# Products of ones in TensorE's order at its waits, in a two-block transformer kernel

## Chip, cores and metric

The kernel runs on one core of one Trainium2 chip. The metric is device time in microseconds of one execution, the median of several. Lower is better. PE stands for TensorE's matmuls, PEld for its weight loads, DVE for VectorE, ACT for ScalarE, POOL for GpSimd.

## Reference

`first_block` runs two layers over x of 512 tokens by 1024, with a context of 256 tokens; `second_block` runs two more layers over the result. Cut to what matters:

```python
# first_block, each layer: RMS norm, mixer, RMS norm, MLP
hx = rms_norm(x, norm1_g) * (1 + mod_x[1]) + mod_x[0]          # hc likewise, 256 context tokens
# layer 0: hybrid_mixer (mLSTM heads and a gated short conv); layer 1: attention_mixer
#   grouped attention: 16 query heads, 4 key and value heads of 64,
#   q and k normed per head and rotated, 512 queries against 256 + 512 keys, softmax, output
x = x + mod_x[2] * y_x
x = x + mod_x[5] * sqrelu_mlp(rms_norm(x, norm2_g) * (1 + mod_x[4]) + mod_x[3], w1, w2)
# second_block, each layer: h = x @ w_in; three branches (latent attention, differential
#   attention, memory attention), each gated and summed; then
x = layernorm(ALPHA * x + merged @ w_out)
x = layernorm(ALPHA * x + square(relu(x @ w1)) @ w2)
```

## The kernel before

All is float32. Activations lie transposed in SBUF, features on the 128 partitions in 8 chunks k, tokens in the columns. A product of float32 accuracy is three products of rounded halves (`mm3`, L1183 to L1185): Hh or Gh with Wh, the same with the low part Wl, and the low part Hl or Gl with Wh. Weights stream in blocks of 1024 columns through two slots; ScalarE rounds each to Wh (L384), GpSimd subtracts to make Wl (L262). `project_block` multiplies a block with a set of token segments.

Each engine has its order of work written out by hand in one program; semaphores tie them. PE takes PSUM banks 0 to 3 in turn: `tiles.take(pe)` waits until VectorE has freed the bank. Banks 4 to 7 have fixed uses. `wait_ready` waits for VectorE's `for_pe`.

The places that the change touches are these.

`rms_stats` sums squares over the features with products of one output column (L1278, L1283), waits for the roots from VectorE and broadcasts them over partitions into banks 4 and 5 (`spread_tokens`, L1240). It runs before the hybrid layer (there with `last_apart` false), before its MLP, before attention, and before the second MLP. `layer_stats` does the same for a layer norm of the second stage, with four column sums (L1230), then `spread(6, shift)` and `spread(4, root)`, each behind a `wait_ready`; it runs twice a layer.

`project_first` follows a norm. It takes its banks, then for each k waits for the normed chunk H from VectorE and ScalarE and multiplies one or two weight blocks with it. It runs eight times: in the hybrid layer, in the four MLPs, at the start of attention, and at the start of the two layers of the second stage.

`attention_pe` works through 4 groups g of 8 turns u. A turn is `scores(g, u)` into banks 4 to 7 (L1593), on odd turns then `output` (weights by values), then `turned_weights(u - 1)`, twelve transposes (L1606). `scores` waits for the exponentials of the turn before (ACT L766), since it writes over the banks that they read. In groups 0 to 2 projections of the next group's keys and queries stand between the turns; in group 3 nothing does. `square_sums(0)` (L1635, L1638) sums squares of keys and queries: it takes a bank, then waits for `raw_done`. It runs once ahead of the groups and at turn 3 of groups 0 to 2.

`onesr` holds ones, 128 by 128, in the rounded type; the hybrid layer uses it for sums.

Of the kernel before, what the change touches and what calls it, by code (L numbers as in the profile page):

```python
# [23 lines left out]
P = 128  # L24
# [306 lines left out]
def latent_scratch(v):  # L331

    M = v["M"]
    kv, kv_sq, q_sq = ([M[:, t * SEQ:(t + 1) * SEQ] for t in ts] for ts in ((0, 1), (2, 3), (4, 5, 6)))
    return kv, kv_sq, q_sq, M[:, 7 * SEQ:8 * SEQ], v["sc"][:, 48:52], v["sc"][:, 52:56]


def layer_norm_scratch(v):

    M, sc = v["M"], v["sc"]  # L340
    scaled = [M[:, i * SEQ:(i + 1) * SEQ] for i in range(KT)]
    return scaled, [sc[:, at:at + 4] for at in (32, 36, 40, 56)], sc[:, 0:8]


def last_squares(v):

    return v["M"][:, 3328:4096]
# [5 lines left out]
    return [M[:, at + TOK * i:at + TOK * (i + 1)] for i in range(3)]  # L353


SINE_TILES = (2, 3, 4, 5)
OUT_ORDER = (4, 5, 0, 1, 2, 3, 6, 7)
CENTRED = ((), (), (), (), (0, 1, 2), (3, 4), (5, 6), (7,))
# [7 lines left out]
def act_program(nc, block, v, n_blocks, extra):  # L366
# [5 lines left out]
    def _(act):  # L372
# [60 lines left out]
        def updated_squares(k, segs):  # L433
            act.wait_ge(for_act, wants.next())
            squares(k, segs)
# [207 lines left out]
        for m in range(KT):  # L643
            used_squared(m, X_SEGS)
            if m < KT - 1:
                updated_squares(m, X_SEGS)
            if m in SINE_TILES:
                t = SINE_TILES.index(m) ^ 1
                act.wait_ge(for_act, wants.next())
# [496 lines left out]
def pe_program(nc, block, v, n_blocks):  # L1146
    Hh, Hl, Gh, Gl, Wh, Wl = (v[n] for n in ("Hh", "Hl", "Gh", "Gl", "Wh", "Wl"))
    Ph, Pl, Qh, Ql, Kh, Kl, Vh, Vl = (v[n] for n in ("Ph", "Pl", "Qh", "Ql", "Kh", "Kl", "Vh", "Vl"))
    psum, S0, S1, M, tab, diag, onesr = (v[n] for n in ("psum", "S0", "S1", "M", "tab", "diag", "onesr"))
# [3 lines left out]
    def _(pe):  # L1153
        tiles = Tiles(v["tile_done"], v["loops_entered"], v["bank_free"])
# [10 lines left out]
        def arriving(width=P):  # L1165

            s = n_block[0] % 2
            n_block[0] += 1
            before = low.next(QUARTERS) - QUARTERS
            return tuple(w[:, s].rearrange("p (k m) -> p k m", m=width) for w in (Wh, Wl)), before  # L1170

        def wait_quarter(before, k):
            pe.wait_ge(v["w_low"], before + k // 2 + 1)
# [4 lines left out]
        def wait_ready(n=1):  # L1178
            pe.wait_ge(v["for_pe"], ready.next(n))

        def mm3(dst, a, b, first, last):

            pe.matmul(dst, a[0], b[0], start=first, stop=False)  # L1183
            pe.matmul(dst, a[0], b[1], start=False, stop=False)  # L1184
            return pe.matmul(dst, a[1], b[0], start=False, stop=last)  # L1185
# [19 lines left out]
        def project_first(*segs_of):  # L1205

            ws = [arriving() for _ in segs_of]
            banks = [[tiles.take(pe) for _ in segs] for segs in segs_of]
            for k in range(KT):
                wait_ready()  # L1210
                for (w, before), segs, bs in zip(ws, segs_of, banks):
                    if k % 2 == 0:
                        wait_quarter(before, k)
                    for b, (t0, n) in zip(bs, segs):
                        mm = mm3(psum[:, b, 0:n], (w[0][:, k, :], w[1][:, k, :]),
                                 (Hh[:, k, t0:t0 + n], Hl[:, k, t0:t0 + n]), k == 0, k == KT - 1)
                        if k == KT - 1:
                            mm.then_inc(v["tile_done"], 1)
# [4 lines left out]
            pe.matmul(psum[0:dst_rows, b, 0:n], lhsT, rhs, start=True, stop=True).then_inc(v["tile_done"], 1)  # L1223

        H, G = (Hh, Hl), (Gh, Gl)

        def column_sums(b, at, x):

            for qt in range(4):
                mm = pe.matmul(psum[:, b, at + qt:at + qt + 1], x[:, qt * P:(qt + 1) * P], ones[:, 0:1], start=True, stop=True)  # L1230
            return mm

        def squares_made():
            pe.wait_ge(v["squared"], squared.next())

        def spread_tokens(bank, col):

            n = col.shape[1]
            for i in range(n):
                mm = pe.matmul(psum[:, bank, i * P:(i + 1) * P], col[:, i:i + 1].broadcast_to([P, P]), ident, start=True, stop=True)  # L1240
            mm.then_inc(v["spread_done"], 1)

        def spread(bank, col):

            wait_ready()
            spread_tokens(bank, col)
# [9 lines left out]
        def layer_stats():  # L1256

            b = tiles.take(pe)
            wait_ready()
            column_sums(b, 0, S0)  # L1260
            wait_ready()
            column_sums(b, 4, S1)
            wait_ready()
            column_sums(b, 8, v["X"][:, KT - 1, X0:TOK])
            squares_made()
            column_sums(b, 12, last_squares(v)).then_inc(v["tile_done"], 1)
            _, (_, shift, _, root), _ = layer_norm_scratch(v)
            spread(6, shift)
            spread(4, root)

        def rms_stats(segs, last_apart=True):

            wait_ready()
            b = tiles.take(pe)
            tt = 0
            for S, (_, n) in zip((S0, S1), segs):
                for i in range(n // P):
                    mm = pe.matmul(psum[:, b, tt:tt + 1], S[:, i * P:(i + 1) * P], ones[:, 0:1], start=True, stop=True)  # L1278
                    tt += 1
            if last_apart:  # L1280
                squares_made()
                for i in range(tt):
                    mm = pe.matmul(psum[:, b, tt + i:tt + i + 1], last_squares(v)[:, i * P:(i + 1) * P], ones[:, 0:1], start=True, stop=True)  # L1283
            mm.then_inc(v["tile_done"], 1)
            wait_ready()
            for lo, hi, c in SPANS[2 - len(segs):]:
                spread_tokens(5 - c, v["sc"][:, 40 + lo // P:40 + hi // P])
# [25 lines left out]
        def mlp(segs, beside=None):  # L1313
            n = len(segs)
            project_first(segs, segs)
            for m in range(2, KT):
                project_block(H, segs)
            with loop(3, 16 * n, 16, KT * n):
                back(segs)
                for m in range(KT):  # L1320
                    project_block(H, segs)
            back(segs, beside)
# [88 lines left out]
        def head_spread(bank, j, done):  # L1411
# [4 lines left out]
            mm.then_inc(done, 1)  # L1416

        rms_stats(ALL_SEGS, False)
        project_first(ALL_SEGS)
        all_head_values()  # L1420
        point, weighed = 0, Count(2 + ML_GIVEN)
        for h in range(ML_HEADS):
# [31 lines left out]
            for group, g0, n in ((0, 0, CTX), (1, X0, SEQ)):  # L1454
# [22 lines left out]
                for step, (kt, dirs) in enumerate(steps + ((None, ""),)):  # L1477
                    if kt is not None:
                        b = tiles.take(pe)
# [39 lines left out]
        for m in range(2, KT):  # L1519
            project_block(G, ALL_SEGS)  # L1520
        rms_stats(ALL_SEGS)
        mlp(ALL_SEGS)

        rms_stats(ALL_SEGS)
        diff_counts = DiffCounts()
        attention_pe(pe, v, tiles, project_block, project_first, mm3, exact, diff_counts)
        wait_ready()
        for m in range(KT):
            project_block(G, X_SEGS)
# [3 lines left out]
        for l in range(2):  # L1533
            _, kv_sq, q_sq, kv_diag, _, _ = latent_scratch(v)
# [31 lines left out]
            for m in range(KT):  # L1566
                project_block(G, X_SEGS, per_k=1 if m == 0 else 0, ks=OUT_ORDER)
                centre(m)
            layer_stats()
            mlp(X_SEGS, centre)  # L1570
            layer_stats()


def attention_pe(pe, v, tiles, project_block, project_first, mm3, exact, counts):
    psum, hand, ident, ones, bones, rot0 = (v[n] for n in ("psum", "hand", "ident", "ones", "bones", "rot0"))
    H, G, Ph, Pl = (v["Hh"], v["Hl"]), (v["Gh"], v["Gl"]), v["Ph"], v["Pl"]
    Qh, Ql, Kh, Kl, Vh, Vl = (v[n] for n in ("Qh", "Ql", "Kh", "Kl", "Vh", "Vl"))
    exp, k32, k2, q_raw, q_sq, v_raw = attention_views(v)[:6]
    keys_scaled = Count()

    def scores(g, u):

        q = slice(u % 4 * P, (u % 4 + 1) * P)
        if g or u:
            pe.wait_ge(v["exps_done"], counts.exps_done.next(2))
        if u % 4 == 0:
            pe.wait_ge(v["operands_ready"], counts.operands_ready.next())
        for c in range(2):
            k = slice(c * HALF, (c + 1) * HALF)
            for i, (x, y) in enumerate(((Qh, Kh), (Qh, Kl), (Ql, Kh))):  # L1590
                for a in range(2):
                    rows = slice(64 * a, 64 * a + 64)
                    mm = pe.matmul(psum[:, 4 + 2 * a + c, 0:HALF], x[rows, q], y[rows, k], start=i == 0, stop=i == 2)  # L1593
                    if i == 2:
                        mm.then_inc(v["scored"], 1)
# [32 lines left out]
    def square_sums(t):  # L1628

        b = tiles.take(pe)  # L1630
        pe.wait_ge(v["raw_done"], counts.raw_done.next(3 if t == 0 else 1))
        at = 0
        if t == 0:
            for tt in range(6):
                pe.matmul(psum[:, b, at:at + 1], k2[:, tt * P:(tt + 1) * P], bones[:, 0:1], start=True, stop=True)  # L1635
                at += 1
        for qt in range(4):
            mm = pe.matmul(psum[:, b, at:at + 2], q_sq[t][:, qt * P:(qt + 1) * P], bones[:, 0:P:64], start=True, stop=True)  # L1638
            at += 2
        mm.then_inc(v["tile_done"], 1)  # L1640
# [1924 lines left out]
```

## Time and profile before

| | |
|---|---|
| median of 3 runs | 4126.87 us (4126.64 to 4128.65) |
| the profiled execution | 4128.24 us, of which 4126.5 us from the first to the last instruction |
| mean granted TensorE clock | 0.973 |
| PE busy | 3920.7 us, 95% of the span |
| PEld, DVE, ACT, POOL busy | 80%, 49%, 36%, 39% |

The granted clock is a share of full speed: 1.00 is 2.4 GHz and 0.50 is 1.2 GHz. A matmul's duration in the rows holds the time in which it overlaps the one before; the distance between starts is its price.

### The profile page before, as it was taken

How to read it: one execution, taken by the hardware profiler on the slowest of the kernel's cores; microseconds unless marked ns; L12 is line 12 of the kernel's file. 1: busy time of each engine (PE TensorE's matmuls, PEld its weight loads, DVE VectorE, ACT ScalarE, POOL GpSimd, SP SyncE). 2: the span in 40 equal slices, each digit the busy share in tenths (PEclk: the TensorE clock that was granted, in tenths of full speed). 3: DMA queues.
4: the chain of work that ended last, by engine and by line, in shares of the span. 5: the costliest groups of instructions: out<-in, count | busy, mean ns of one | idle time of the engine just before them, and what ended most of it. 6: DMA issues, size and time to landing. Idle time of an engine off the chain costs nothing.

```text
span 4126.5 us, 58926 instructions
## 1 busy us (share of the span) xinstructions
PE 3920.7 (95%) x20508; PEld 3307.5 (80%) x20508; DVE 2031.4 (49%) x3318; ACT 1495.4 (36%) x2438; POOL 1628.2 (39%) x2044
## 2 busy tenths in 40 slices
PE   7999899999988889999999999999989999999998
PEld 6888799999977668887677788788867777887887
DVE  5566652332457763335837723532467475225225
ACT  3222231111245542223636633322255465333222
POOL 2111133433321025665242355565632423545665
PEclk9999999999989989999999999999999999999999
DMA  4433211111110012222121122222211211222222
GB/s 174 145 137 138 85 60 67 62 66 61 57 36 21 16 44 92 97 97 93 41 77 57 57 92 94 75 97 97 93 61 43 80 52 60 101 90 77 97 97 97
DMA packets 92744, 328.26 MB, mean 80 GB/s; under 512 B 10240, under 2 KB 12544, under 8 KB 92544
## 3 DMA queue, kind: packets, MB, share of 16 engines
q1 hardware_dynamic: 90928, 323.61, 22.3%
q8 instruction: 135, 2.21, 0.2%
q10 hardware_dynamic: 1616, 1.90, 0.2%
q14 instruction: 65, 0.53, 0.0%
HBM read 323.38 MB, written 2.10 MB: 79 GB/s over the span
## 4 chain that ended last, share of the span: by engine, by line
issue 60%; POOL 30%; PE 8%; DVE 1%; POOLq 1%; ACT 0%; DVEq 0%
POOL Wl L262 30%; PE psum L1183 3%; PE psum L1184 3%; PE psum L1185 3%; POOLq L257 0%; POOLq L259 0%; DVE S L2068 0%; DVE M L2246 0%; DVE X L2068 0%; DVE X L2202 0%; PE psum L1230 0%; PE psum L1240 0%; DVE X L2263 0%; POOLq L262 0%; ACT hand L394 0%
## 5 line engine op out<-in xcount | busy, mean ns | idle before, releaser
L262 POOL TENSOR_TENSOR Wl<-raw,Wh 128x256 fp32r<-128x256 f32 x2040 | 1628.0, 829 | 2491.9 <-ACT Wh L384 2491.4
L384 ACT ACTIVATE Wh<-raw 128x1024 fp32r<-128x1024 f32 x510 | 539.9, 1059 | 1595.9 <-PE psum L1185 1573.8
L1183 PE MATMUL psum<-Hh,Wh 128*128 128x512 f32 (+1 forms) x2704 | 1034.2, 382 | 43.7 <-DVEq L2111 16.8
L1184 PE MATMUL psum<-Hl,Wh 128*128 128x512 f32 (+1 forms) x2704 | 1014.3, 375 | 0.0
L1185 PE MATMUL psum<-Hh,Wl 128*128 128x512 f32 (+1 forms) x2704 | 1014.1, 375 | 0.0
L1183 PE MATMUL psum<-Gh,Wh 128*128 128x512 f32 (+3 forms) x2032 | 747.7, 368 | 12.9 <-DVE Gl L2756 4.6
L1185 PE MATMUL psum<-Gh,Wl 128*128 128x512 f32 (+3 forms) x2032 | 742.9, 366 | 0.0
L1184 PE MATMUL psum<-Gl,Wh 128*128 128x512 f32 (+3 forms) x2032 | 742.7, 365 | 0.0
L1183 PEld LDWEIGHTS psum<-Hh,Wh 128*128 128x128 f32 x2704 | 518.4, 192 | 147.9 <-issue 50.9
L1185 PEld LDWEIGHTS psum<-Hh,Wl 128*128 128x128 f32 x2704 | 516.9, 191 | 71.7
L1184 PEld LDWEIGHTS psum<-Hl,Wh 128*128 128x128 f32 x2704 | 518.9, 192 | 67.9 <-issue 1.3
L1183 PEld LDWEIGHTS psum<-Gh,Wh 128*128 128x128 f32 (+1 forms) x2032 | 381.2, 188 | 71.8 <-DVEq L2111 8.3
L1185 PEld LDWEIGHTS psum<-Gh,Wl 128*128 128x128 f32 (+1 forms) x2032 | 381.1, 188 | 51.4
L1184 PEld LDWEIGHTS psum<-Gl,Wh 128*128 128x128 f32 (+1 forms) x2032 | 381.3, 188 | 50.0 <-issue 0.5
L2068 DVE TENSOR_TENSOR hand<-hand 128x512 f32<-128x512 f32 (+1 forms) x160 | 111.6, 698 | 433.1 <-ACT hand L394 415.7
L2267 DVE SCALAR_TENSOR_TENSOR X<-psum,mod,X 128x256 f32<-128x256 f32 (+1 forms) x160 | 83.9, 548 | 341.4 <-PE psum L1185 340.2
L2263 DVE SCALAR_TENSOR_TENSOR X<-X,psum 128x512 f32<-128x512 f32 x64 | 44.0, 687 | 244.9 <-PE psum L1185 243.8
L2297 DVE TENSOR_TENSOR Gl<-hand,Gh 128x512 fp32r<-128x512 f32 (+1 forms) x160 | 155.4, 971 | 5.5
L2077 DVE CAST Gh<-hand 128x512 fp32r<-128x512 f32 (+1 forms) x160 | 117.7, 736 | 5.5
L2068 DVE TENSOR_TENSOR S<-psum,hand 128x512 f32<-128x512 f32 x32 | 22.1, 692 | 196.2 <-PE psum L1185 195.7
L985 ACT ACTIVATE stage<-psum,soft 128x512 f32<-128x512 f32 x128 | 86.7, 686 | 73.6 <-DVE soft L3144 73.6
L394 ACT ACTIVATE hand<-psum 128x512 f32<-128x512 f32 (+3 forms) x180 | 90.4, 525 | 33.6 <-DVEq L2114 29.6
(353 smaller groups left out, 4489.4 us busy)
## 6 DMA issues: line engine op xcount, KB each, us to landing
raw<-in_wstream SPq DMA_DIRECT2D x510, 512.0 KB, 3.2
stage<-in_ada SPq DMA_DIRECT2D x80, 512.0 KB, 4.1
M<-in_ada SPq DMA_DIRECT2D x16, 512.0 KB, 5.3
X<-in_xT SPq DMA_DIRECT2D x1, 2048.0 KB, 15.1
out<-X SPq DMA_DIRECT2D x8, 256.0 KB, 2.0
X<-in_ctxT SPq DMA_DIRECT2D x1, 1024.0 KB, 10.3
M<-in_memT ACTq DMA_DIRECT2D x1, 1024.0 KB, 5.8
M<-in_axial ACTq DMA_DIRECT2D x1, 512.0 KB, 5.6
```

Of the source, the lines that this page charges most:

```text
L262: pool.tensor_tensor(Wl[:, s, c], raw[:, s, c], Wh[:, s, c].bitcast(F32), ALU.subtract).then_inc(w_low, 1)
L384: act.activation(Wh[:, s], raw[:, s], ACT.Copy).then_inc(v["w_high"], 1)
L394: last = act.activation(hand[p, s, cols], one, func, **k)
L985: last = act.activation(stage[:, s, c * SEQ:(c + 1) * SEQ], psum[:, 4 + 2 * j + c, :], ACT.Exp, bias=soft[:, 4 * j + c:4 * j + c + 1], acc ...
L1183: pe.matmul(dst, a[0], b[0], start=first, stop=False)
L1184: pe.matmul(dst, a[0], b[1], start=False, stop=False)
L1185: return pe.matmul(dst, a[1], b[0], start=False, stop=last)
L2068: do(dve.tensor_tensor(dst, x, y, op))
L2077: do(dve.tensor_copy(dst, x))
L2263: last = dve.scalar_tensor_tensor(out=X[:, m, t0:t0 + n], in0=X[:, m, t0:t0 + n], scalar=1.0, in1=psum[:, b, 0:n], op0=ALU.mult, op1=ALU.add)
L2267: last = dve.scalar_tensor_tensor(out=X[:, m, lo:hi], in0=psum[:, b, lo - t0:hi - t0], scalar=mod[:, part, m, c:c + 1], in1=X[:, m, lo:hi] ...
L2297: do(dve.tensor_tensor(Gl[:, m, t0:t0 + w], r, Gh[:, m, t0:t0 + w].bitcast(F32), ALU.subtract))
```

## The change

A helper issues n products of ones with ones, 512 columns each, into a bank whose content is written anew before anybody reads it. Nobody reads them. Calls stand in PE's order at these places: after the sums of squares in `rms_stats` (4, when `last_apart`), between the two broadcasts of `layer_stats` (3), in `project_first` behind the taking of the banks and ahead of the first wait for H (7), in `square_sums(0)` behind the taking of the bank (5), ahead of the first scores (12), and ahead of the scores of turn 1 of group 0 and of the odd turns of group 3 (6). In the last kind they first wait until the next bank is free. No wait and no other instruction is removed or moved.

```diff
+CLOCK_ROOTS, CLOCK_SHIFTED, CLOCK_NORMED, CLOCK_SCORES, CLOCK_SQUARES = 4, 3, 7, 6, 5
...
             banks = [[tiles.take(pe) for _ in segs] for segs in segs_of]
+            keep_clock(banks[0][0], CLOCK_NORMED)
             for k in range(KT):
                 wait_ready()
...
+        def keep_clock(bank, n):
+
+            for _ in range(n):
+                pe.matmul(psum[:, bank, :], onesr[:], onesr[:].unsqueeze(1).broadcast_to([P, 4, P]), start=True, stop=True)
...
             spread(6, shift)
+            keep_clock(4, CLOCK_SHIFTED)
             spread(4, root)
...
             mm.then_inc(v["tile_done"], 1)
+            if last_apart:
+                keep_clock(5, CLOCK_ROOTS)
             wait_ready()
...
+    def next_bank():
+
+        b = tiles.at % 4
+        pe.wait_ge(tiles.free[b], tiles.uses[b].base + tiles.uses[b].k + 1)
+        return b
+
     def scores(g, u):
 
         q = slice(u % 4 * P, (u % 4 + 1) * P)
+        if g == 3 and u % 2 or (g, u) == (0, 1):
+            keep_clock(next_bank(), CLOCK_SCORES)
         if g or u:
             pe.wait_ge(v["exps_done"], counts.exps_done.next(2))
+        elif u == 0:
+            keep_clock(4, 2 * CLOCK_SCORES)
...
         b = tiles.take(pe)
+        if t == 0:
+            keep_clock(b, CLOCK_SQUARES)
         pe.wait_ge(v["raw_done"], counts.raw_done.next(3 if t == 0 else 1))
```

## Rows read from the trace of the kernel before

**Rows 1.** The page: granted TensorE clock in 40 equal slices, in tenths.

```profile
PEclk9999999999989989999999999999999999999999
```

**Rows 2.** PE in order of time, second stage: start, us, instruction [idle before].

```profile
1901.09 0.39 PE L1185 MATMUL psum<-Gh,Wl 128*128 128x512 f32 x1
1901.32 0.39 PE L1183 MATMUL psum<-Hh,Wh 128*128 128x512 f32 x1
...
1960.79 0.67 PE L1223 MATMUL psum<-S,const 96*96 96x512 f32 x1 [2.06 <-ACT S L894]
...
3072.08 1.37 PE L1223 MATMUL psum<-S,const 96*96 96x512 f32 x2 [2.07 <-ACT S L894]
...
3074.09 0.63 PE L1185 MATMUL psum<-Ph,Wl 128*128 128x512 f32 x1
3074.52 0.63 PE L1183 MATMUL psum<-Ph,Wh 128*128 128x512 f32 x1
```

**Rows 3.** PE's waits over the span: us in total, times, longest us.

```profile
PE psum L1593 <- ACT stage L766: 15.0, 5, 3.5
```

**Rows 4.** Windows in attention: us, PE busy (records), clock, DMA.

```profile
1427.49:1435.98 8.49, 8.49 (x44) 0.80 0.01 2
1442.68:1452.06 9.38, 9.38 (x44) 0.71 0.00 0
1458.09:1466.56 8.47, 8.47 (x44) 0.80 0.01 3
1472.59:1482.36 9.77, 9.77 (x42) 0.68 0.00 0
1226.02:1232.96 6.94, 6.94 (x43) 1.00 0.10 35
...
1176.00:1181.00 5.00, 5.00 (x18) 0.50 0.01 3
1212.60:1226.00 13.40, 13.39 (x72) 0.87 0.00 1
```

**Rows 5.** PE in order of time, in attention.

```profile
1175.65 0.69 PE L1593 MATMUL psum<-Kh,Qh 64*128 64x384 f32 x2 [5.71 <-DVE Ql L2902]
...
1189.13 0.44 PE L1593 MATMUL psum<-Kh,Qh 64*128 64x384 f32 x2
...
1212.61 1.50 PE L1635 MATMUL psum<-const,tab 128*128 128x1 f32 x12 [1.43 <-DVE Gl L2108]
...
1427.49 0.67 PE L1593 MATMUL psum<-Kh,Qh 64*128 64x384 f32 x2 [2.38 <-ACT stage L766]
...
1442.68 0.69 PE L1593 MATMUL psum<-Kh,Qh 64*128 64x384 f32 x2 [3.50 <-ACT stage L766]
```

**Rows 6.** Windows in the latent branch, columns as in rows 4.

```profile
1960.00:1970.00 10.00, 7.83 (x39) 1.00 0.12 45
1963.12:1967.30 4.18, 3.00 (x21) 1.00 0.00 0
```

**Rows 7.** VectorE in order of time, at three places.

```profile
1426.25 1.29 DVE L2108 TENSOR_TENSOR Gl<-psum,Gh 128x512 fp32r<-128x512 f32 x2
...
588.44 2.44 DVE L2171 SCALAR_TENSOR_TENSOR Hl<-M,mod,Hh 128x256 fp32r<-128x256 f32 x4
...
1556.07 1.65 DVE L2171 SCALAR_TENSOR_TENSOR Hl<-M,mod,Hh 128x512 fp32r<-128x512 f32 x2
```

**Rows 8.** Windows from first to last product of project_first, columns as in rows 4.

```profile
575.83:595.11 19.28, 19.28 (x96) 0.86 0.00 1
1547.79:1561.80 14.01, 14.00 (x48) 0.78 0.19 57
...
2634.02:2649.08 15.06, 14.30 (x48) 0.83 0.00 1
...
3746.22:3761.28 15.06, 14.46 (x48) 0.81 0.00 0
```

**Rows 9.** PE in order of time, between two broadcasts of a layer norm.

```profile
3741.47 2.08 PE L1240 MATMUL psum<-const,sc 128*128 128x128 f32 x8 [0.60 <-DVEq L2111]
```

More of the change, by code:

```diff
@@ L1525, in _ @@
         diff_counts = DiffCounts()
-        attention_pe(pe, v, tiles, project_block, project_first, mm3, exact, diff_counts)
+        attention_pe(pe, v, tiles, project_block, project_first, mm3, exact, diff_counts, keep_clock)
         wait_ready()
@@ L1571, in _, with attention_pe @@
             layer_stats()
-def attention_pe(pe, v, tiles, project_block, project_first, mm3, exact, counts):
+def attention_pe(pe, v, tiles, project_block, project_first, mm3, exact, counts, keep_clock):
     psum, hand, ident, ones, bones, rot0 = (v[n] for n in ("psum", "hand", "ident", "ones", "bones", "rot0"))
```

## Prediction

> **What bounds the kernel now.** I read the page first, then the waits of TensorE (PE), then PE's order of time with the granted clock beside it. PE is busy nearly all the time, and the row of its clock shows no digit but 8 and 9 [rows 1]. The mean grant of 0.973 means that some 2 x 0.027 x 4126.5 = 223 us of the span ran at the lower of the two levels, 1.2 GHz, 0.50 in the records, and the rest at 2.4 GHz. At the lower level a product of 512 columns starts 0.43 us after the one before it, at the upper one 0.22 to 0.23 us [rows 2], so I take 0.225 us for a filler at full clock, 0.43 at half clock, and 1 - 0.225/0.43 = 0.48 us for each busy microsecond at half clock as its price. The price is paid only where PE is what the next step waits for. The clock falls behind waits of PE; the longest repeated one in attention is the wait of the scores for the exponentials, 15.0 us in five waits [rows 3]. So the reader is to see three things at each place where fillers stand: is there a wait before which they stand, does the clock stay up with them, and would PE's speed behind the wait have mattered.
>
> **Attention, last group, odd turns (four places, six fillers each).** From the scores to the end of the transposes behind them PE runs without a stop. With the same work and the clock at 1.00 this takes 6.94 us; the four turns in question take 8.49, 9.38, 8.47 and 9.77 us at clocks of 0.68 to 0.80 [rows 4]. Their prices are 1.55, 2.44, 1.53 and 2.83 us, 8.35 in all, and they count in full: what follows (evictions, maxima, exponentials, next odd turn) starts from the last transposes. Six fillers take 6 x 0.225 = 1.35 us, well inside the 3.50 us of the second place [rows 5]; the third and fourth waits have the same form. They leave some 2.0 to 2.15 us idle. Is that short enough? The nearest rows disagree: after a wait of 2.06 us the clock stayed at 1.00, after one of 2.07 us the products came 0.43 us apart [rows 2, 6]. So the fall is not abolished, it is made rarer: of the 6.8 us of these three I take three fifths, 4.1, with bounds of 0 and 6.8. The first place differs. Its fillers first wait for a bank, which VectorE frees with the first of its two L2108 subtractions, at about 1426.25 + 0.65 = 1426.9 [rows 7]; six fillers from there end at 1428.3, and the scores could have gone at 1427.49 [rows 5]. Cost 0.8, gain 1.55 (bounds 0 and 1.55).
>
> A page of the Trainium skill speaks against this part. Transposes, says "TensorE: Matmul & The Clock Gate", Part 4, do not count as PE activity as other products do. By that rule the idle time here would be longer by the 1.5 to 2 us of transposes ahead of the wait, and the clock would fall as before: the gain of 4.1 would be nothing. The trace does not bear it out, since a stretch of 4.18 us of nothing but transposes and a wait had a clock of 1.00 [rows 6].
>
> **Attention, opening scores (12 fillers).** They take 2.7 of the 5.71 us [rows 5] and leave 3.0, too long to hold the clock in most cases, but the low stretch should begin later. 5 us and more behind the wait were at 0.50 [rows 4], worth 2.4; I take half, 1.2 (0 to 2.4).
>
> **Attention, second turn (six fillers).** The scores at 1189.13 follow the projection without a wait [rows 5]. The fillers stand in PE's way: 1.35 us lost, and the exponentials of this turn are what the next scores wait for.
>
> **Attention, square sums (five fillers, four places).** The fillers stand behind the wait for the bank. In three of the four places that is the wait that ends last (1.43 us, ended by VectorE's L2108 freeing the bank [rows 5]); nothing is left to hide them: 3 x 5 x 0.225 = 3.4 us lost. Behind it the clock is 0.87 over 13.4 us [rows 4], that is 3.5 us at half clock, 1.7 us of price, some 5 us for three places. The fillers break an idle stretch with narrow products behind it; I take half, 2.5 (0 to 5). The first of the four stands in a real wait, but narrow products and another long wait follow, and I put it at 0.
>
> **Norms ahead of project_first (seven fillers, eight places; four more in the three RMS norms).** Here what matters is who sets the pace. In the MLP after the first block the last H is ready at 588.44 + 2.44 = 590.88 [rows 7]; a hop of 0.25 and 12 products of 384 columns follow. 96 of them took 19.28 us at 0.86 [rows 8], 5.4 us of it low; 13.9 + 5.4/1.91 = 16.7, or 0.174 each at full clock. So it could end at 593.2 instead of 595.11: 1.9 us. In the next MLP, 1557.72 + 0.25 + 6 x 0.225 = 1559.3 instead of 1561.80: 2.5 us. I take both whole, 4.4 (0 to 4.4), because the four fillers, the spread products and the seven fillers together make PE dense from the sums on, and the clock can be back before the projection. The broadcasts in the three RMS norms may run partly at full clock: 0.9 us (0 to 3). The other places give nothing. In the second stage the projection is paced by VectorE: 15.06 us at a clock of 0.83 and 15.06 at 0.81 [rows 8], each with waits at its end that take up what the slow start lost; the attention's and the first one are of that kind. And the first latent projection of the second stage has no wait at all: L1183 on H follows L1185 on G after 0.23 us [rows 2], so its seven fillers are a loss of 7 x 0.225 = 1.6 us.
>
> **Layer norms (three fillers, four places).** Between the two broadcasts PE waits 0.60 us in the best of the four cases [rows 9], and the eight records of one take 2.08 us. I read that as half clock, since only narrow products ran for some 6 us before. Three fillers at 0.43 are 1.29 us, so each time the second broadcast is 0.7 to 1.3 us late; I take 0.9, 3.6 in all; the last of the four goes straight into the kernel's tail. The denser work may bring the clock back within the second broadcast: I take 1.8 (0 to 3.6).
>
> **Sum.** Gains 4.1 + 1.55 + 1.2 + 2.5 + 4.4 + 0.9 + 1.8 = 16.45. Costs 0.8 + 1.35 + 3.4 + 1.6 + 3.6 = 10.75. Net 5.7 us faster. The profiled execution took 4128.24 us (span 4126.5), 1.4 above the median of 4126.87; taken from the median this is 4121.
>
> **Rivals.** *Everything is kept (4111).* Each row of fillers is enough to hold or to restore the clock: the gains take their upper ends, 1.55 + 6.8 + 2.4 + 5 + 4.4 + 3 + 3.6 = 26.75, less 10.75 is 16.0. For it: one wait of 2.06 us that did no harm. Against it: the one of 2.07 that did. *Gains and costs cancel (4127).* A stretch at half clock need not move with the work: if work starts 1 us sooner and the stretch ends when it would have ended anyway, that 1 us is run at half clock and about half of the gain is gone again. Then some two thirds of the gains remain, 10.75 of 16.45. For it: many low stretches of the same length behind waits of 1.4 to 3.5 us. *Slower (4137).* Products of ones with ones, whose result is the same each time, do not hold the clock; then only the costs are left, 10.75 us, at the places with no wait. It decides from the point at which less than 2.5 us of the gains come true. For it: no row shows such products alone in a wait. Against it: nothing in the rows ties the grant to values rather than to columns that move.
>
> **How the numbers follow.** My forecast, a gain of 2 to 12 us, has 0.52; everything kept 0.22; cancelled 0.13; slower 0.09; something unseen 0.04. A measurement here tells about 0.2% from nothing, 8.25 us, so the line is at 4118.6. Two fifths of the forecast's chance lie beyond it, 0.21; with the first rival that is 0.43 for faster. Slower by that much: the last rival and half of the unseen, 0.11. Within it: 0.46. The range of 4110 to 4129 takes in the forecast, the first two rivals, and the spread that the moments of the falls bring.
>
> **What would show it.** Right: turns of the last group near 7 us from scores to transposes in most but not all of the three later places, and the first with its scores later than now behind the bank; the MLP projections ending 1.3 to 1.6 us after the last H but for the hop; fillers without a wait ahead of them at the first latent projection, at the second turn and behind three bank waits; the second stage's projections still 15.06 us long. Wrong: the clock at 1.00 through all of attention's last group and the layer norms (4111), or 0.50 behind waits filled with fillers just as before (4137).

## Result and profile after

The changed kernel takes 4142.74 us, median of ten runs (4135.52 to 4147.0); the kernel before, beside it, 4128.84 us (4126.64 to 4131.99). The ratio is 1.0031, 95% interval 1.0023 to 1.0039: 12.8 us slower (9.5 to 16.1), by more than the 0.2% set as the line. The forecast was 4121, the range 4110 to 4129.

The page after: span, busy times, granted clock and the queue of instructions; then one group of TensorE's (PE's) waits.

```profile
span 4140.5 us, 59206 instructions
PE 3953.4 (95%) x20650; PEld 3324.3 (80%) x20650; DVE 2026.4 (49%) x3318; ACT 1495.8 (36%) x2438; POOL 1629.1 (39%) x2044
PEclk8999999999999999999999999999999999999999
q8 instruction: 154, 2.52, 0.3%
```

```profile
PE psum L1613 <- ACT stage L767: 7.8, 4, 2.2
```

The wait of the scores for the exponentials fell from 15.0 us [rows 3] to 7.8, and the mean clock went from 0.973 to 0.974. The row to stop at is the fourth: queue q8 carries instructions, and it moved 154 packets instead of 135. (Before, its row on the page is "q8 instruction: 135, 2.21, 0.2%": packets, MB, share.)

To see where the time went I took the start of the same product in both profiled executions and subtracted. These are the differences (after less before), in us, by the place in the kernel before:

| up to | what lies there | change | sum |
|---|---|---|---|
| 560 | hybrid layer | +0.5 | 0.5 |
| 620 | first MLP's norm and projection | -1.0 | -0.5 |
| 1100 | its hardware loop | +8.9 | 8.4 |
| 1186 | attention up to the opening scores | -3.3 | 5.1 |
| 1240 | second turn, first square sums in the groups | +3.0 | 8.1 |
| 1420 | groups 0 to 2 | -2.6 | 5.5 |
| 1545 | group 3, output projection | +1.2 | 6.6 |
| 1600 | second MLP's norm and projection | -1.9 | 4.8 |
| 1902.5 | first latent projection | +1.6 | 6.4 |
| 2615 | rest of the first layer's branches | -0.2 | 6.3 |
| 2656 | layer norm 1 | +2.1 | 8.4 |
| 3020 | layer norm 2 | +2.1 | 10.5 |
| 3730 | second layer's branches | -0.8 | 9.7 |
| 3766 | layer norm 3 | +2.3 | 12.0 |
| 4113 | layer norm 4 | +2.1 | 14.1 |

The largest term is at a place that the prediction does not name. PE in order of time at the end of the loop's first and second trip, after the change (start, us, instruction, idle before it):

```profile
778.62 0.34 PE L1186 MATMUL psum<-Hh,Wl 128*128 128x384 f32 x1
781.80 0.44 PE L1184 MATMUL psum<-Gh,Wh 128*128 128x384 f32 x1 [2.84 <-POOL Wl L262]
...
783.02 0.52 PE L1184 MATMUL psum<-Gh,Wh 128*128 128x384 f32 x1
```

```profile
919.08 0.44 PE L1184 MATMUL psum<-Gh,Wh 128*128 128x384 f32 x1 [2.31 <-POOL Wl L262]
```

L1186 is the last product of the loop's body, L1184 on G its first: TensorE stands still for 2.84 and 2.31 us at the jump back, 137 us apart, and from 783.0 to 786.2 the products then start 0.32 us apart instead of 0.17. GpSimd is named as the releaser, but it had finished that block's Wl at 775.4 (771.81 + 3.57), so it was something that the semaphores do not show.

```profile
771.81 3.57 POOL L262 TENSOR_TENSOR Wl<-raw,Wh 128x256 fp32r<-128x256 f32 x4 [4.67 <-ACT Wh L385]
```

The queue of instructions in this stretch, before and after (packets, MB, share):

```profile
q8 instruction: 1, 0.02, 0.0%
```

```profile
q8 instruction: 19, 0.31, 0.5%
```

These are the rows for 770 to 1060 us. Before, code came for the first trip, and then a single packet at 1045 us, at the end of the third: both jumps back were passed without any. After, all three trips fetched theirs.

### The profile page after: what moved, and what is told of

It reads as the page before. It is cut to its first block, busy times and chain, and to the rows that moved or that the text cites. A ratio compares the mean times of both kernels' runs of the same rounds, so it can differ in the third digit from the quotient of the medians.

```text
span 4140.5 us, 59206 instructions
## 1 busy us (share of the span) xinstructions
PE 3953.4 (95%) x20650; PEld 3324.3 (80%) x20650; DVE 2026.4 (49%) x3318; ACT 1495.8 (36%) x2438; POOL 1629.1 (39%) x2044
## 3 DMA queue, kind: packets, MB, share of 16 engines
q8 instruction: 154, 2.52, 0.3%
## 4 chain that ended last, share of the span: by engine, by line
issue 60%; POOL 30%; PE 8%; DVE 1%; POOLq 1%; ACT 0%; DVEq 0%
POOL Wl L262 30%; PE psum L1184 3%; PE psum L1186 3%; PE psum L1185 3%; POOLq L257 0%; POOLq L259 0%; DVE S L2090 0%; DVE M L2268 0%; PE psum L1247 0%; PE psum L1237 0%; DVE X L2090 0%; DVE X L2224 0%; DVE X L2285 0%; POOLq L262 0%; ACT hand L395 0%
## 5 line engine op out<-in xcount | busy, mean ns | idle before, releaser
L1184 PE MATMUL psum<-Hh,Wh 128*128 128x512 f32 (+1 forms) x2704 | 1027.3, 380 | 33.7 <-DVEq L2133 9.3
L1186 PE MATMUL psum<-Hh,Wl 128*128 128x512 f32 (+1 forms) x2704 | 1006.6, 372 | 0.0
L1184 PE MATMUL psum<-Gh,Wh 128*128 128x512 f32 (+3 forms) x2032 | 750.5, 369 | 17.6 <-POOL Wl L262 9.3
L1186 PE MATMUL psum<-Gh,Wl 128*128 128x512 f32 (+3 forms) x2032 | 745.5, 367 | 0.0
L1184 PEld LDWEIGHTS psum<-Hh,Wh 128*128 128x128 f32 x2704 | 512.3, 189 | 146.9 <-issue 28.0
L1186 PEld LDWEIGHTS psum<-Hh,Wl 128*128 128x128 f32 x2704 | 511.7, 189 | 70.8
L1184 PEld LDWEIGHTS psum<-Gh,Wh 128*128 128x128 f32 (+1 forms) x2032 | 383.0, 188 | 77.2 <-POOL Wl L262 9.1
L1186 PEld LDWEIGHTS psum<-Gh,Wl 128*128 128x128 f32 (+1 forms) x2032 | 382.8, 188 | 51.8
```

## Experiments

A packet of q8 is 2.52 MB / 154 = 16.4 KB. The loop's body in the built program has 768 products of two instructions each and 91 others, 1627 in all. Code that is fetched in blocks can touch one block more or less according to where it begins. 36 instructions, 18 products with their weight loads, stand ahead of this loop in the change. The Trainium skill ("Advanced Engine Details and Errata", ISA Cache) gives blocks of 16 KB with 256 instructions and room for 128 KB of them on TensorE; the size of the packets agrees, and by it the body is six blocks and 91 instructions. This is where the blocks of 256 in the expectations come from. All ratios below are to the kernel before, run beside each.

**1. Nothing but place.** Edit to the kernel before:

```diff
+        for _ in range(36):
+            pe.sem_inc(v["pad"], 1)
         pe.wait_ge(v["consts_loaded"], 32)
```

> The kernel before, with 36 instructions more at TensorE's very start (each adds 1 to a semaphore that nobody waits for; TensorE waits 6.8 us there anyway). That is as many instructions as the 18 products of ones with their weight loads that stand ahead of the first MLP's hardware loop in the changed kernel. No product of ones anywhere. Theory A (place of the code): the loop's body now straddles one more block of 16 KB, is fetched anew in each of its three trips (packets of the instruction queue q8 between 756 and 1045 us, where the kernel before has none), TensorE stands still for 2 to 3 us at both back-edges and half clock follows; 7 to 9 us slower than before, about 4136. Theory B (the products themselves, or weights that come late behind them, make the gaps): nothing changes, within 1 us of before, no q8 packets in the loop.

1.0011 (1.0002 to 1.0020), 4.5 us slower. q8 moved 19 packets between 770 and 1060 us, and PE stood still at both jumps:

```profile
784.53 0.60 PE L1184 MATMUL psum<-Gh,Wh 128*128 128x384 f32 x1 [2.80 <-POOL Wl L263]
...
922.11 0.43 PE L1184 MATMUL psum<-Gh,Wh 128*128 128x384 f32 x1 [2.60 <-POOL Wl L263]
```

The loop is 7.6 us longer than before in this trace, without one product of ones in the kernel. Theory B falls. The median is 4.5 us slower where A said 7 to 9, though the interval reaches to 8.3 us.

**2. All products, moved by a block.** The changed kernel with two such rows of 110 increments.

> The changed kernel with 220 such instructions more, 110 at TensorE's start and 110 in its 7.7 us wait for a transfer at 13 us; with the 36 of the 18 products that makes 256, one block of 16 KB, so that the first MLP's loop lies in its blocks as it did before. Theory A: the two gaps at the back-edges (2.84 and 2.31 us) and the half clock behind them are gone; 7 to 9 us faster than the changed kernel, about 4134, still 5 us slower than before through the layer norms. Theory B: no change, 4142.

1.0065 (1.0051 to 1.0078), 26.9 us slower. The loop is as before (0.0 us of change, no packet in its second and third trip), but the increments cost 18 us: the first product starts at 17.87 us instead of 6.81, and the one behind the wait for a transfer at 37.60 instead of 20.65. So the fetches and the gaps follow the place of the code; the time says little.

**3. No products in the layer norms.** `CLOCK_SHIFTED` 0.

> The changed kernel without the three products between the two broadcasts of the four layer norms. Theory A (these three run at half clock in the way of the second broadcast, 1.3 us each time less the 0.2 to 0.6 us of wait there): 0.7 to 1.3 us in each of four places, 3 to 5 us faster than the changed kernel, about 4138.5. Theory B (the loss of 2.0 to 2.6 us per layer norm is theirs alone): 8 to 10 us faster, about 4133.5. Theory C (it is the earlier fall of the clock that costs, by its phase): less than 1 us.

1.0014 (1.0005 to 1.0023): 5.8 us slower than before instead of 12.8, so 7.0 us for the twelve products, between A and B. The two intervals allow some 2 to 12 us, so the time alone does not tell A from B; the traces say more. First layer norm of the changed kernel:

```profile
2626.82 0.95 PE L1237 MATMUL psum<-const,S 128*128 128x1 f32 x8
...
2630.14 1.87 PE L1237 MATMUL psum<-const,X 128*128 128x1 f32 x8 [0.71 <-DVEq L2133]
...
2634.64 2.08 PE L1247 MATMUL psum<-const,sc 128*128 128x128 f32 x8 [0.93 <-DVEq L2133]
2636.36 1.63 PE L1232 MATMUL psum<-onesr 128*128 128x512 f32 x3
2637.79 1.91 PE L1247 MATMUL psum<-const,sc 128*128 128x128 f32 x8
```

And the same norm in a kernel without the three (the eighth below), where the clock fell at the same sums:

```profile
2614.68 0.94 PE L1238 MATMUL psum<-const,S 128*128 128x1 f32 x8
...
2617.99 1.87 PE L1238 MATMUL psum<-const,X 128*128 128x1 f32 x8 [0.71 <-DVEq L2134]
...
2622.49 3.78 PE L1248 MATMUL psum<-const,sc 128*128 128x128 f32 x16 [0.92 <-DVEq L2134]
```

From the first sum to the end of the broadcasts it is 2639.70 - 2626.82 = 12.88 us with them and 2626.27 - 2614.68 = 11.59 without: 1.29 us, three times 0.43, none of it hidden. A further 1 us comes with the moment at which the clock falls (a share of C): third sums of 1.87 us are at half clock, of 1.05 at full. In the profile of the changed kernel it fell there in all four norms, in that of before in none of them fully. In the other traces, with and without the three products, it was a mixture.

**4. Only attention.** The other counts are 0.

> The changed kernel with only its products in attention (12 ahead of the first scores, 6 ahead of the second turn's and of the four odd turns of the last group, 5 ahead of the square sums); none in the norms. Nothing stands ahead of the first MLP's loop. Theory A (attention gains a little, the loop's place and the norms cost): 1 to 2 us faster than before, about 4127, no q8 packets in the loop. Theory B (attention's gains are eaten by its costs, as in my rival): 0 to 3 us slower than before.

1.0005 (0.9996 to 1.0014), 2 us slower, nearer B, though the interval holds no change as well. In the loop one packet, as before.

**5. No products in layer norms, none ahead of the loop.** `normed` and `roots` are counts per call of `project_first` and `rms_stats`, in the program's order.

```diff
+        normed, roots = [0, 0, 7, 7, 7, 7, 7, 7], [0, 4, 4]
-            keep_clock(banks[0][0], CLOCK_NORMED)
+            keep_clock(banks[0][0], normed.pop(0))
-                keep_clock(5, CLOCK_ROOTS)
+                keep_clock(5, roots.pop(0))
```

> The changed kernel without the three products in the layer norms (as in the third experiment) and without the 18 ahead of the first MLP's loop (7 in the hybrid layer, 4 and 7 at the first MLP). Theory A (the loop's code, +7.6 to +8.9 us in three traces that have it fetched anew): no q8 packets between 757 and 1047 us, no gap at the back-edges; against the third experiment 8.5 us less, plus 1.0 us for the gain at the first MLP's start that is given up: 1.0014 becomes 0.9996, about 2 us faster than before. Theory B (the loop's gaps were of a chance kind, or cost less in the run without a profile): no change against the third experiment, about 6 us slower than before.

1.0009 (1.0000 to 1.0018), 3.7 us slower. A was right about packets (one, as before) and gaps (none) and wrong about the time: 2 us less than the third instead of 7.5, with intervals of 3.7 us either way on both. The trace shows a loop 8.5 us shorter than the third's. That the fetches cost less in the median than in the profiled execution, as Theory B also allowed, is not ruled out.

**6. Only the places that could pay.**

```diff
+        normed, roots = [0, 0, 7, 7, 0, 0, 0, 0], [0, 4, 4]
-        if g == 3 and u % 2 or (g, u) == (0, 1):
+        if g == 3 and u in (3, 5, 7):
-        if t == 0:
-            keep_clock(b, CLOCK_SQUARES)
```

> As the kernel above, and also without the products that stand where TensorE waits for nothing, or behind the wait that ends last: square sums, second turn, the first odd turn of the last group, and all of the second stage. Left are 12 ahead of the first scores, 6 ahead of turns 3, 5 and 7 of the last group, and 4 and 7 at attention's norm and the second MLP's. Theory A (square sums and second turn cost 2.7 to 3.6 us, the first latent projection 1.6, each the same in every trace that has them): 4.3 to 5 us faster than the kernel above, 6 to 7 us faster than before, ratio 0.9985. Theory B (what they hold of the clock pays for them, as I had put the square sums' gain at 2.5): the same as the kernel above within 2 us.

0.9998 (0.9989 to 1.0007): 4.5 us less than the fifth, as A said; not faster than before, where A said 6 to 7 us. A part of the miss may be in the trace: nothing stands ahead of the loop, yet its first jump back (and not its second) had a gap of 2.65 us with nine packets of q8 more than before, 4.5 us in all. I take it that the kernel before lies on the border itself.

**7. The sixth with the first MLP's products** (`normed` [0, 7, 7, 7, 0, 0, 0, 0], `roots` [4, 4, 4]).

> As the kernel above, with the 4 and 7 products of the first MLP's start as well: 22 instructions ahead of its loop instead of none (36 straddled a block more). One look at the queue of code. Theory A: if the loop had more than 22 instructions of room in its blocks, no q8 packets in it and 1.0 us gained at the MLP's start; if less, the packets and 7.6 to 8.9 us lost. Theory B (the loop's gaps have nothing to do with where its code lies): the gaps do not follow the packets.

4131.4 us in its one run. Packets in all trips, gaps of 2.63 and 2.64 us at the jumps, the loop 9.0 us longer, the MLP's start 1.0 us shorter: 22 instructions are too many.

**8. The sixth with twelve products** (`2 * CLOCK_SCORES`) at turns 3, 5 and 7.

> As the sixth experiment, with 12 instead of 6 products ahead of the scores of turns 3, 5 and 7 of the last group: 2.7 us and more of the 3.5 us wait. Theory A (products of ones count like others, the idle rest of 1.85 us behind six of them is what lets the clock fall in some turns): with less than 0.9 us idle all three turns run at full clock, 7 us from scores to transposes, 0 to 2 us faster than the sixth. Theory B (they do not hold the clock): half clock behind them as often as before, no gain. Theory C (twelve are too many, since the wait is not 3.5 us each time): the scores start late by up to 1 us a turn, 0 to 3 us slower.

0.9992 (0.9983 to 1.0001). The windows of these turns, from the scores on (us, then busy time of PE, PEld, DVE, ACT and POOL, clock, DMA), after the change and then here, where the first also holds 0.65 us of waiting at its end:

```profile
1451.25:1459.71 8.46, 8.46 (x43) 6.75 (x43) 6.23 (x14) 3.82 (x8) 0.00 (x0) 0.80 0.00 0
1465.80:1472.69 6.89, 6.89 (x42) 5.68 (x42) 5.33 (x13) 3.29 (x7) 0.00 (x0) 1.00 0.00 1
1479.09:1487.60 8.51, 8.47 (x42) 6.88 (x42) 5.84 (x13) 3.41 (x8) 0.00 (x0) 0.80 0.00 0
```

```profile
1441.24:1448.85 7.61, 6.96 (x42) 5.71 (x43) 6.05 (x14) 4.20 (x9) 0.00 (x0) 1.00 0.00 0
1455.14:1462.04 6.90, 6.89 (x43) 5.68 (x44) 5.34 (x13) 3.31 (x7) 0.00 (x0) 1.00 0.00 1
1468.45:1475.50 7.05, 6.94 (x42) 5.66 (x42) 5.49 (x13) 3.48 (x8) 0.00 (x0) 1.00 0.01 2
```

```profile
1451.63 3.00 PE L1233 MATMUL psum<-onesr 128*128 128x512 f32 x12
1455.14 0.44 PE L1614 MATMUL psum<-Kh,Qh 64*128 64x384 f32 x2 [0.51 <-ACT stage L767]
```

The scores are not late and all three turns are at 1.00. The median is 2.5 us below the sixth's, which the intervals do not tell from none. Over the traces of this study the three turns took 9.0 us on average without products (twelve turns, none under 8.4), 7.5 with six (sixteen of 24 at about 7.0, the rest at 8.4 to 8.6), and 7.0 with twelve (six of six).

**9 and 10. The loop put past the border.** The eighth with the first MLP's products and 85 increments; the kernel before with 108.

```diff
+        for _ in range(40):
+            pe.sem_inc(v["pad"], 1)
         pe.wait_ge(v["consts_loaded"], 32)
...
+            for _ in range(45 if q == 2 else 0):
+                pe.sem_inc(v["pad"], 1)
             ada_products(q)
```

> The kernel of the eighth experiment with the 4 and 7 products of the first MLP's start (22 instructions) and 85 increments of a semaphore that nobody waits for (40 at TensorE's start, 45 in its wait for a transfer at 13 us): the loop's code lies 107 instructions further than before. The loop's body has 1627 instructions, 6 blocks of 256 and 91 more. Theory A (22 and 36 further it touches one block more than fits; before, it ends right at the end of a block, which is why one trace of six without anything ahead of it, the sixth experiment's, fetched code for one trip; more than 91 further it begins in the next block and fits again): no q8 packets in the loop in this place, and the 1.0 us of the MLP's start is kept: 1 us less than the eighth experiment, ratio 0.9988, 0.9980 to 0.9996. Theory B (every shift costs the fetches): q8 packets in all trips, 8 us slower than that, 1.0009.

0.9992 (0.9983 to 1.0001), the same as the eighth and within what A gave. No gap at the jumps and no packet in the second and third trip, 107 instructions further on; the MLP's start 0.9 us shorter in the trace.

> The kernel before with 108 such increments (40 at the start, 48 at 13 us, 20 in the hybrid layer behind the taking of the banks, ahead of the wait for H) and no product of ones. Theory A: no q8 packets in the loop, and never a trip with them; the increments lie in waits, so the same time as before within 2 us, or 1 to 2 us less if before pays for such trips now and then. Theory B: packets in all trips, 8 us slower.

1.0005 (0.9996 to 1.0014). No gap at the jumps and no packet in the second and third trip; 2 us slower, at the edge of what was expected, and no gain.

**11. Eight increments.**

> The kernel before with 8 such increments at TensorE's start. One look at the queue of code. Theory A (the loop's end touches the end of a block before): q8 packets in the loop already with 8, and 4 to 9 us lost at the back-edges. Theory B (the border lies between 8 and 22): none, and the sixth experiment's one trip was of another cause.

4137.85 us in its one run. Theory A holds at its sharpest: 19 packets between 770 and 1060 us, and these two gaps.

```profile
781.05 0.44 PE L1184 MATMUL psum<-Gh,Wh 128*128 128x384 f32 x1 [2.64 <-POOL Wl L263]
...
918.72 0.68 PE L1184 MATMUL psum<-Gh,Wh 128*128 128x384 f32 x1 [2.71 <-POOL Wl L263]
```

The loop is 10.2 us longer. From 1140 to 4113 us the difference to the trace of the kernel before stays between 9.2 and 9.6 us: with eight instructions that take about a microsecond, in a wait, this one execution is 9.6 us longer than the profiled one of before.

**12. The changed kernel, whole, past the border** (the 85 increments of the ninth).

> The changed kernel, all its 142 products of ones kept, with 85 increments (40 at the start, 45 at 13 us, where they lie in waits) so that the first MLP's loop lies 121 instructions further than before instead of 36: past the 91 that straddle. Theory A: no q8 packets in the loop; 7.6 to 10.2 us less than the changed kernel's 12.8 above before: ratio 1.0006 to 1.0013, median about 4.5 us above before. Theory B (the second experiment's 18 us of increments hid that the fetches cost little in unprofiled runs): as the changed kernel, 1.003.

1.0016 (1.0007 to 1.0025): 6.6 us slower than before instead of 12.8. That is 6.2 us for the place of the code (the two intervals allow some 1 to 11), somewhat under A's 7.6 to 10.2; the ratio ended just above A's 1.0006 to 1.0013. The increments may not be quite free: the four traces with 36 to 108 of them (first, ninth, tenth, twelfth) are 2.2 to 4.3 us behind before's at 560 us, the seven others without any lie between -0.9 and +2.7. The queues between 770 and 1060 us, where the one packet comes behind the loop:

```profile
q1 hardware_dynamic: 5037, 18.34, 19.0%
q8 instruction: 1, 0.02, 0.0%
```

By distance from where the loop lay before: 0 instructions, five traces, no fetch at the jumps but for one trip; 8, 22 and 36, five traces, all trips fetched, 7.6 to 10.2 us lost; 107, 108, 121 and 256, four traces, none. The border can be seen in the first trip itself. Here is q8 in it, before (646.2 to 779.2 us) and after (645.7 to 778.8):

```profile
q8 instruction: 6, 0.10, 0.3%
```

```profile
q8 instruction: 7, 0.11, 0.4%
```

All eight traces without a gap have six packets in the first trip (before, the last at 755.5 us), all six with a gap have more (after, the seventh at 772.2). The sixth experiment's trace has its seventh at 776.7 us, 2 us ahead of the jump, and is the one that fetched for one trip only.

## Why the prediction was wrong

In short: the sum priced a product of ones by its time on PE alone, and had no term for what 18 of them do to the place of the code behind them; and it took gains at the layer norms and the square sums that did not come.

**What it left out: +8.9 in the trace.** The step that failed first is the price of a filler, "I take 0.225 us for a filler at full clock, 0.43 at half clock": it takes the price as time on PE and nothing else. An instruction also has a place in a stream. The two gaps (5.15 us) and the half clock behind each (3.4 us at 0.32 instead of 0.17 us a product, some 1.6 us lost each time) make 8.3 of the 8.9. In the medians the same effect is smaller: 4.5 us (the first), about 2 or 3 (the third against the fifth) and 6.2 (the twelfth), each within several us. No term and no rival held it, and without it the time would still have been slower: 6.6 us (the twelfth).

**Layer norms: a net cost of 1.8 forecast, 4.0 to 5.2 from the products.** The cost per norm was 1.29 where the clock had fallen by the sums and some 0.7 where it had not (experiment 12 has two of each: broadcasts ending 12.88 and 11.51 us after the first sum, against 11.60 and 10.6 to 11.0 without), so 3.6 was low by a tenth or more. The failed step is "The denser work may bring the clock back within the second broadcast: I take 1.8". Where the clock had fallen by the sums, the second broadcast took 1.91 us in all four norms of the changed kernel (1.76 at best, in the second experiment), and 1.91 or 1.92 without the products. A further 1 us a norm in the profiled execution is the earlier fall.

**Square sums and second turn: a net cost of 2.25 forecast, 4.8 measured.** From 1186 to 1420 us the six traces that have these products lose 3.0 us against the trace of before on average, the eight without (before counted, at 0) win 1.8, though these scatter between a loss of 0.1 and a win of 6.9. The costs (3.4 and 1.35) are there: five products take 1.27 us behind the bank's wait, as at 1217.79, and the second turn came to 1.4 to 2.2 us in the six traces, more than its 1.35.

```profile
1217.79 1.43 PE L1232 MATMUL psum<-onesr 128*128 128x512 f32 x5 [1.41 <-DVE Gl L2130]
1219.06 1.90 PE L1657 MATMUL psum<-const,tab 128*128 128x1 f32 x12
...
1222.60 0.69 PE L1613 MATMUL psum<-Kh,Qh 64*128 64x384 f32 x2
```

The gain of 2.5, "The fillers break an idle stretch with narrow products behind it", is not to be seen in the sum: here the scores behind are at half clock all the same. It is not nothing everywhere. At the second of the three places all six traces have won back 1.4 to 1.9 us within 12 us of their products, since the sums behind ran at full clock; but so did two of the eight without products, by themselves.

**Last group: 4.85 forecast net, some 1.5 kept.** In the three later turns the mechanism was right, even in its share: "made rarer", with three fifths taken, and two thirds measured; 1.57 us a turn or 4.7 for three, against 4.1. What the prediction made of the rule on transposes, a gain of nothing, did not come; the rule itself is not tested, since the products of ones stand between the transposes and the rest of the wait. In the first odd turn the scores came 1.9 to 2.0 us behind the work before them in five of the six traces with products, against 1.8 to 2.4 without, so the cost of 0.8 did not show; in the sixth (the third experiment) they came 4.3 us behind. Its clock was 1.00 in five of six with products, but also in three of eight without. And from the start of group 3 to 1545 us the ten traces with products average -0.6 us and the four without (before counted) +0.9, so about 1.5 us remain of the turns' gain. In all ten the clock falls behind the last turn, around the output projection; in the profile of before it does not, though in two of the other three it does. That looks like the second rival's mechanism, a stretch that does not vanish but moves, which I had priced too low; no run tested it by itself.

**MLP starts: 4.4 and 0.9 for the broadcasts forecast, about 2.1.** 1.0 at the first in all traces that have the products; at the second 1.8 against 0.7 in the traces without, so 1.1. The clock came back as forecast, to 1.00 in both projections (0.86 and 0.78 before); what failed is the end of the sum, "a hop of 0.25 and 12 products" behind the last H. The first projection ended 3.3 us behind it (594.63 against 591.37), since its products ran without a stop from 590.18, before that H was there. At attention's norm nothing can be told (-1.1 to +1.7). **Opening scores: 1.2 forecast, nothing that can be told:** ten traces with products average -1.1, four without -0.7, with -3.3 to +1.2 and -2.4 to 0.0 as extremes.

**First latent projection: 1.6 forecast, 1.6 in each of five traces, 0.0 in each without.** The row to read:

```profile
1906.12 1.77 PE L1232 MATMUL psum<-onesr 128*128 128x512 f32 x7
1907.73 0.40 PE L1184 MATMUL psum<-Hh,Wh 128*128 128x512 f32 x1
```

**Sum, with sizes as measured.** Gains 1.5 + 2.1 = 3.6; costs 8.9 + 4.8 + 1.6 + 4.6 = 19.9; 16 us slower by terms, 14.1 in the profile, 12.8 (9.5 to 16.1) in the runs. The "slower" rival (4137) had the right sign with the wrong cause: products of ones do hold the clock, in six turns of six with twelve of them. The forecast that the second stage's projections would stay paced by VectorE held: the one behind the first layer norm begins 8.15 us later than before and ends 8.4 later, and takes 15.3 us at a clock of 1.00 where it took 15.06 at 0.83.

**Open.** What decides the moment of a fall is not settled. Kernels with nothing in attention differ there by up to 7 us from the profile before, so a term under 2 us cannot be read from one pair of traces. Nor is it settled why the fetches cost less in the medians than the 7.6 to 10.2 us of the profiled executions. Why one block more makes all of them come anew was not tried. That a block beyond the jump is read ahead would explain it, and the sixth experiment's single trip with its late seventh packet; it fits the packets of the first trip, but is only argued.

## What to carry to other kernels

An instruction put ahead of a large hardware loop (a loop that the engine runs itself, by a jump back in its code) can cost more than it takes: compare the packets of the instruction queue in the loop before and after, and if there are new ones, move the loop by cheap instructions in a wait before judging the change. Put products that keep the clock only in waits that are longer than they are, on the path, and fill the wait nearly whole (twelve, of 3.0 us in a wait of 3.5, did it each time, six in two cases of three). Even then allow for a low stretch behind the next wait: the best versions here came to 3.3 us less than before (0.9983 to 1.0001), which is not told from none.

## What the runs showed of the hardware

- A loop of 1627 instructions on TensorE passed its two jumps back without a packet of code, or fetched its code anew in each trip with 2.2 to 2.8 us of standstill per jump and half clock behind, according to its place; eight instructions ahead of it decided (the eleventh, one run).
- An increment of a semaphore takes TensorE some 0.14 to 0.16 us: 110 of them at its start put the first product at 17.87 us, and 110 more made a gap of 15.15 us (the second).
- A product of ones with ones counts for the clock: of the three later odd turns of the last group none in twelve ran wholly at full clock without such products, six in six with twelve of them.
